# A decoder trunk's PEER layers: from gathered experts to both expert tables streamed through TensorE

## The chip, the core and the metric

The kernel runs on one core of a Trainium2 chip. A core has TensorE (PE in the rows: matrix products, with a separate weight-load stream PEld), VectorE (DVE), ScalarE (ACT), GpSimd (POOL) and SyncE (SP, which here only issues transfers), each with a queue of its own, and 16 DMA engines. SBUF is the on-chip memory of 128 partitions; PSUM is where TensorE leaves its products. The metric is device microseconds (us) of one execution, the median of several. The measurement can tell about 0.2% from no change.

## What is computed

A two-layer decoder trunk over 256 tokens of width 1024, all in float32. Layer 0 mixes tokens by sparse attention and retention, layer 1 by a convolution module; both are followed by a PEER block, and a last norm ends the trunk. PEER holds 16384 experts of one neuron each: a row of `u` (in) and a row of `v` (out), both 1024 wide.

```python
def peer_ffn(h, w_q, sub_keys, u, v):
    q = (xf @ w_q).reshape(T, P_HEADS, 2, P_QDIM // 2)          # T = 256, 8 heads, 2 x 128
    s1 = jnp.einsum('thd,kd->thk', q[:, :, 0], sub_keys[0])      # 128 keys each
    s2 = jnp.einsum('thd,kd->thk', q[:, :, 1], sub_keys[1])
    v1, i1 = lax.top_k(s1, 16); v2, i2 = lax.top_k(s2, 16)
    cand = (v1[..., :, None] + v2[..., None, :]).reshape(T, P_HEADS, 256)
    sv, ci = lax.top_k(cand, 16)
    eidx = (e1 * 128 + e2)                                       # 128 picks of a token
    gate = softmax(sv)
    hb = jnp.einsum('td,tkd->tk', xb, u[ib])
    act = jax.nn.gelu(hb) * gb
    return jnp.einsum('tk,tkd->td', act, v[ib])
```

Each token uses 128 experts of the 16384 in each layer (256 x 128 = 32768 picks a layer).

## The kernel before

The program is written engine by engine, with semaphores between them; the order on each engine is the order of the code. Tokens are worked in two tiles of 128 (`TILES`), and the PEER work in four phases `p`: layer 0 tile 0, layer 0 tile 1, layer 1 tile 0, layer 1 tile 1.

- **Picks.** `queries` (L1243) multiplies a head's 1024x256 slice of `wq` (loaded into `wbuf`, two buffers of 1 MB) with the transposed tokens `h_t`; ACT copies it to `q_t`; `scores` (L1254) multiplies with the keys; DVE's `heads` (L807) takes the top 16 of both score rows, the top 16 of their 256 sums, and turns them into expert numbers `eidx` and gates. One call of `heads` treats a pair of heads of one tile.
- **Experts.** `ring` holds 16 gathered rows for each token, 8 KB each (`u` and `v` side by side). GpSimd's `gathers` (L383) issues 512 indirect transfers (4 phases x 128 picks), each of one row for each of 128 tokens. DVE's `expert_round` (L879) makes the dot product with `u` (`dot`, L888) and adds half of the `v` row into `x_tok` (`add_v`, L896). ACT makes GELU times gate and a diagonal matrix of it (L558, L562, L569); TensorE adds the other half of the `v` row with that diagonal matrix (L1280).
- **Around it.** The heads of the next phase and layer 1's convolution for one tile are laid between expert rounds on every engine (`conv_pair`, L922, on DVE: 31 taps for each of 8 groups of 128 channels; `conv_beside` on PE and ACT). The output products of layer 0's tile 1 stand between rounds too (L1339). A norm is a square and a root on ACT, a multiplication by root and gain on DVE (L659, the gain row is loaded in 128 copies), a transposition on PE (L1027) and a copy on ACT (L431).
- **The start.** SP issues x, the first gain row, the parts of `w_in`, small tables, then `keys_sb` and `chan_sb` (L288, L289). PE's `product` (L1035) is a chain of 8 matmuls that add up over 1024 inputs.

In the rows a float32 matmul of the program appears as two records: 512 issued at L1280 are listed as x1024.

## Time and profile before

| | |
|---|---|
| median of 3 runs | 1693.82 us (1692.57 to 1694.78) |
| the profiled execution | 1694.12 us, of which the span of its core 1692.4 us |
| busy share of the span | DVE 84%, PE 58%, POOL 45%, PEld 35%, ACT 29% |
| moved | 625.78 MB, mean 370 GB/s; 536.90 MB of it gathered rows |
| granted TensorE clock, mean | 0.786 of full |

The profile has a page and views of the trace. The busy line gives each engine's share; the strips cut the span into 40 slices, a digit for each (9 is 90% or more, or nine tenths of the clock); the chain of work that ended last is followed back from the last instruction, step by step to what released it, so it says which engine set the time; the groups are instructions of one line and shape. The timeline lists instructions in order of time, merged when they are alike: start, length, engine, line, operation, count. For matmuls the length of a merged row includes the last one's way through the array, so the rate is read from start to start.

### The profile page before, as it was taken

To read this page: it belongs to the slowest core of one execution; us is meant where nothing else is said; L and a number is where in the kernel's file an instruction comes from. 1 tells how busy PE (TensorE), PEld (TensorE's weight loads), DVE (VectorE), ACT (ScalarE), POOL (GpSimd) and SP (SyncE) were. 2 spreads that over 40 slices of the span, in tenths; PEclk is the share of its full clock that TensorE was granted. 3 is DMA by queue.
4 is the path that set the end of the run, shared out by engine and by line. 5 is a ranking of instruction groups with operands and counts; after the bars stand their busy time and mean duration, and the time that the engine had idled before them with its cause. 6 is when DMAs were issued, how large, how long until landed. Compare 5 with 4: busy or idle time off the path is not lost.

```text
span 1692.4 us, 17116 instructions
## 1 busy us (share of the span) xinstructions
PE 983.0 (58%) x3934; PEld 597.7 (35%) x3934; DVE 1428.2 (84%) x3330; ACT 498.5 (29%) x1442; POOL 758.1 (45%) x565
## 2 busy tenths in 40 slices
PE   7999765444554634577444564557654446566555
PEld 7786443222331422344222342334332222122122
DVE  2755889999998989887999999986899999777776
ACT  2221332222223423333222333323332223232222
POOL 0002544433434587743433367734444336445541
PEclk9999877677777866798677787779877778877777
DMA  9146999999999978899999988889999989999996
GB/s 373 43 147 255 416 421 421 421 397 417 381 385 399 421 294 352 345 422 421 385 381 407 415 346 337 352 332 421 409 380 383 384 344 417 422 422 423 422 422 257
DMA packets 87274, 625.78 MB, mean 370 GB/s; under 512 B 9648, under 2 KB 10416, under 8 KB 12720
## 3 DMA queue, kind: packets, MB, share of 16 engines
q0 software_dynamic: 73728, 536.90, 77.7%
q1 hardware_dynamic: 13488, 88.20, 12.9%
q8 instruction: 24, 0.39, 0.1%
q14 instruction: 34, 0.28, 0.0%
HBM read 624.02 MB, written 1.05 MB: 369 GB/s over the span
## 4 chain that ended last, share of the span: by engine, by line
DVE 45%; PE 22%; DMA 14%; issue 11%; ACT 4%; DVEq 3%; ACTq 1%; POOL 0%; POOLq 0%
DVE ring L888 15%; DMA ring<-experts_dram,idx_now 12%; DVE x_tok L896 10%; PE side L1280 9%; PE pm L1038 8%; DVE conv_buf L939 7%; PE side L1038 2%; ACT act_v L562 1%; DMA wbuf<-w_dram 1%; DVE top_i L821 1%; DVE rest L822 1%; DVE top_i L834 1%; DVE best_i L840 1%; DVE side L843 1%; ACTq L565 1%
## 5 line engine op out<-in xcount | busy, mean ns | idle before, releaser
L410 POOL DMA_INDIRECT ring<-experts_dram,idx_now x512 | 728.0, 1422 | 680.0 <-DMA ring<-experts_dram,idx_now 309.6
L1280 PE MATMUL side<-ring,diag 128*128 128x512 f32 x1024 | 593.0, 733 | 598.7 <-ACT diag L569 598.5
L888 DVE SCALAR_TENSOR_TENSOR ring<-ring,h_tok 128x1024 f32<-128x1024 f32 x512 | 616.7, 1222 | 55.4 <-DMA ring<-experts_dram,idx_now 50.2
L1280 PEld LDWEIGHTS side<-ring,diag 128*128 128x128 f32 x1024 | 231.0, 237 | 904.7 <-ACT diag L569 668.5
L896 DVE SCALAR_TENSOR_TENSOR x_tok<-ring,act_v,x_tok 128x512 f32<-128x512 f32 x512 | 384.6, 751 | 26.1 <-ACT act_v L562 20.3
L558 ACT ACTIVATE ge<-hb 128x4 f32<-128x4 f32 x128 | 26.3, 205 | 696.6 <-DVE ring L888 696.6
L569 ACT ACTIVATE diag<-ident,act_v 128x128 f32<-128x128 f32 x512 | 163.8, 390 | 15.9 <-issue 2.3
L939 DVE SCALAR_TENSOR_TENSOR conv_buf<-conv_buf,chan_sb 128x128 f32<-128x128 f32 x480 | 126.7, 348 | 0.0
L1038 PEld LDWEIGHTS side<-h_t,wbuf 128*128 128x128 f32 x1024 | 119.3, 192 | 15.4 <-issue 15.4
L1038 PE MATMUL side<-h_t,wbuf 128*128 128x128 f32 x1024 | 119.5, 275 | 0.0
L562 ACT ACTIVATE act_v<-ge,gates 128x1 f32<-128x1 f32 x512 | 109.0, 283 | 15.5 <-issue 11.5
L393 POOL COPY idx_now<-eidx 128x16 uint32 x32 | 23.9, 745 | 170.8 <-DVE x_tok L896 97.0
L549 ACT ACTIVATE expo<-lead 128x16 f32<-128x16 f32 x32 | 6.7, 208 | 190.9 <-DVE lead L849 190.9
L1038 PEld LDWEIGHTS pm<-h_t,wbuf 128*128 128x128 f32 x512 | 59.7, 192 | 7.8 <-issue 7.8
L558 ACT ACT_TABLE_LOAD x46 | 59.0, 1283 | 3.4 <-issue 2.5
L1038 PE MATMUL pm<-h_t,wbuf 128*128 128x128 f32 x512 | 59.7, 275 | 0.0
L1038 PE MATMUL pm<-conv_buf,ring 128*128 128x128 f32 x448 | 53.7, 280 | 0.2 <-DVE ring L766 0.2
L1038 PEld LDWEIGHTS pm<-conv_buf,ring 128*128 128x128 f32 x448 | 52.3, 194 | 1.4 <-DVE ring L766 0.6
L1032 PE MATMUL pm<-ident,h_tok 128*128 128x128 f32 x56 | 12.8, 409 | 57.5 <-DVE h_tok L659 57.5
L888 DVE DVE_READ_ACCUMULATOR ring<-ring,h_tok 128x1 f32 x512 | 43.3, 85 | 0.0
L818 DVE MAX8 top_v<-side 128x8 f32<-128x128 f32 x64 | 15.6, 288 | 26.8 <-PE side L1259 26.8
L1038 PE MATMUL pm<-ring,conv_buf 128*128 128x512 f32 (+2 forms) x128 | 36.8, 445 | 1.1 <-ACT conv_buf L433 1.1
(188 smaller groups left out, 796.7 us busy)
## 6 DMA issues: line engine op xcount, KB each, us to landing
wbuf<-wq_dram SPq DMA_DIRECT2D x32, 1024.0 KB, 9.3
wbuf<-w_dram SPq DMA_DIRECT2D x24, 1024.0 KB, 9.5
ring<-w_in_dram SPq DMA_DIRECT2D x5, 2048.0 KB, 22.8
wbuf<-w_o_dram SPq DMA_DIRECT2D x8, 1024.0 KB, 8.3
ring<-experts_dram,idx_now POOLq DMA_INDIRECT x512, 11.5
gain<-gains_dram SPq DMA_DIRECT2D x7, 512.0 KB, 12.9
ring<-w_in_dram SPq DMA_DIRECT2D x1, 1696.0 KB, 9.8
x_tok<-x_dram SPq DMA_DIRECT2D x2, 512.0 KB, 4.8
```

The source lines that it names most:

```text
L393: pool.tensor_copy(idx_now[:, half, :], eidx[:, t, ds(i * (2 * RING) + half * RING, RING)]) \
L410: pool.indirect_dma_start(ring[:, r, :], None, table[layer], bass.IndirectOffsetOnAxis(idx_now[:, half, r:r + 1], 0)) \
L558: act.activation(ge[:, c], hb[:, c], ACT.Gelu)
L562: last = act.activation(act_v[:, r:r + 1], ge[:, r:r + 1], ACT.Copy, scale=gates[:, t, ds(i * RING + r, 1)])
L565: act.drain()
L569: act.activation(diag[:, (b % 2) * BATCH + j, :], ident[:, :], ACT.Copy, scale=act_v[:, r:r + 1]).then_inc(diag_ready, 1)
L821: dve.max_index(top_i[:, b, j, 0:8], top_v[:, b, j, 0:8], side[b, j])
L888: dve.scalar_tensor_tensor(out=ring[:, r, 0:D], in0=ring[:, r, 0:D], scalar=1.0, in1=h_tok[:, t, :], op0=ALU.mult, op1=ALU.mult, accum_out ...
L896: dve.scalar_tensor_tensor(out=xs, in0=ring[:, r, D:D + HALF], scalar=act_v[:, r:r + 1], in1=xs, op0=ALU.mult, op1=ALU.add).then_inc(v_add ...
L939: step = dve.scalar_tensor_tensor(out=dst, in0=src, scalar=tap, in1=dst, op0=ALU.mult, op1=ALU.add)
L1038: last = pe.matmul(dst, lhs(k), rhs(k), start=(k == 0), stop=(k == KD - 1))
L1280: pe.matmul(acc, diag[:, r % (2 * BATCH), :], ring[:, r, D + HALF:2 * D], start=False, stop=(last and r == RING - 1)) \
```

## The change

The phases are gone. A layer now takes its 256 tokens together, and all 16384 experts are evaluated for all of them. Expert number is e1 x 128 + e2; the tables are laid out on the host by e2.

- **U.** `expert_inputs`: 64 chunks of 1 MB a layer, each with the `u` rows of two values of e2 for all 128 values of e1. 16 matmuls (2 x 8, weights 128x128 of the table, 256 tokens moving) give 2 x 128 experts for 256 tokens in one PSUM bank; ACT applies GELU into `act`, which has a value for every expert and token (128 KB a partition).
- **Picks to gates.** DVE's `heads` now takes one head of both tiles; e1, e2 and the gate go to `picks`, are transposed once a layer (`transpose_picks`), and for each group of 8 tokens DVE builds one-hot matrices of e1 (`hot1`, 8x128) and of half the values of e2 (`hot2`, 8x64), GpSimd multiplies `hot2` by the gates, PE multiplies the two for each token (`gates_of_experts`: 8 matmuls of 64 moving columns, written to every 8th column of a PSUM bank), and DVE multiplies the result into `act` (`apply_gates`). A layer has 2 halves x 32 groups.
- **V.** `expert_outputs`: 64 chunks of 1 MB a layer, 8 matmuls each (2 tiles x 2 values of e2 x 2 halves of 512 columns, weights from `act`), added up in four PSUM banks over the layer; DVE adds them to `x_tok`.
- **Moved.** The convolution module treats 256 tokens at once and stands between the two PEER blocks with nothing beside it; the output products of tile 1 stand ahead of PEER. Gains are applied after the transposition, from `chan_sb` (one column for each 128 channels, L566), by DVE where ACT copied before. `chan_sb` is loaded second, `keys_sb` after all parts of `w_in`, and both add to the semaphore `small_loaded`. Weights and tables stream through `stream`, four buffers of 1 MB.

```diff
-    def gathers(p): ...                                     # 512 indirect DMAs
-    def expert_round(p, i, ...): ...                        # DVE, ACT and PE
+            def keep_h_t(e, dst):
+                dve.wait_ge(h_t_ps, e + 1)
+                g = CP_NORM + e // 2 * KD
+                dve.tensor_tensor(dst, norm_at(e).rearrange("p (k c) -> p k c", k=KD),
+                                  chan_sb[:, g:g + KD].unsqueeze(2).broadcast_to([P, KD, P]), ALU.mult).then_inc(h_t_ready, 1)
...
             norm(0)
             norm(1)
+            dve.wait_ge(small_loaded, 32)
+            keep_h_t(0, h_in[0])
+            keep_h_t(1, h_in[1])
...
+            def one_hots(i, half, g):
+                n = (2 * i + half) * GROUPS + g
+                if n >= 2:
+                    dve.wait_ge(gate_ps, n - 1)
+                dve.tensor_tensor(hot1[n % 2], iota..., picks_t[:, 0, tok]..., ALU.is_equal).then_inc(hot1_ready, 1)
+                dve.tensor_tensor(hot2[n % 2], iota..., picks_t[:, 1, tok]..., ALU.is_equal).then_inc(hot2_ready, 1)
...
+            def expert_inputs(i, c):
+                n = i * E_CHUNKS + c
+                w = chunk(C_U[i] + c).rearrange("p (k e c) -> p k e c", k=KD, e=E2_CHUNK)
+                if n >= 2:
+                    pe.wait_ge(gelu_ready, n - 1)
+                for e in range(E2_CHUNK):
+                    last = product(u_at[n % 2][:, e * TOKENS:(e + 1) * TOKENS], lambda k: w[:, k, e, :], lambda k: h_t[:, k, :])
+                last.then_inc(u_ps, 1)
...
+            def gates_of_experts(i, half, g):
+                n = (2 * i + half) * GROUPS + g
+                pe.wait_ge(hot1_ready, n + 1)
+                pe.wait_ge(gated_ready, n + 1)
+                if n >= 2:
+                    pe.wait_ge(gate_done, n - 1)
+                dst = gate_at[n % 2].rearrange("p (e u) -> p u e", u=GROUP)
+                for u in range(GROUP):
+                    last = pe.matmul(dst[:, u, :], hot1[n % 2][:, u, :], hot2[n % 2][:, u, :], start=True, stop=True)
+                last.then_inc(gate_ps, 1)
...
+            def expert_outputs(i, c):
+                for t in range(TILES):
+                    for e in range(E2_CHUNK):
+                        for k in range(2):
+                            last = pe.matmul(v_at[t][k], act[:, c * E2_CHUNK + e, t * P:(t + 1) * P], w[:, e, k * 512:(k + 1) * 512], ...)
...
+            def peer(i):
+                pe.wait_ge(h_t_ready, 4 + 4 * i)
+                queries(i, 0)
+                for h in range(1, P_HEADS):
+                    queries(i, h)
+                    scores(i, h - 1)
+                scores(i, P_HEADS - 1)
+                for c in range(E_CHUNKS // 2):
+                    expert_inputs(i, c)
+                transpose_picks(i)
+                for c in range(E_CHUNKS // 2, E_CHUNKS):
+                    expert_inputs(i, c)
+                    if c > E_CHUNKS // 2:
+                        gates_of_experts(i, 0, c - E_CHUNKS // 2 - 1)
+                gates_of_experts(i, 0, GROUPS - 1)
+                pe.wait_ge(gate_done, (2 * i + 1) * GROUPS)
+                for c in range(E_CHUNKS // 2):
+                    expert_outputs(i, c)
+                    gates_of_experts(i, 1, c)
+                pe.wait_ge(gate_done, (2 * i + 2) * GROUPS)
+                for c in range(E_CHUNKS // 2, E_CHUNKS):
+                    expert_outputs(i, c)
```

On DVE `peer(i)` is: eight `heads`, `normalise_gates` (waits for one Exp on ACT, which ACT has behind the GELU of chunk 31), the wait for the transposed picks, then for each half and group `one_hots` of the next group and `apply_gates` of this one.

On PE, where layer 0's experts begin, the program before has the diagonal products (L1280) with head work and output products (`pm<-wbuf,conv_buf`) between them:

```order
L1280 MATMUL side<-ring,diag 128x512 x4
L1038 MATMUL side<-h_t,wbuf 128x128 x16
L1280 MATMUL side<-ring,diag 128x512 x4
L1038 MATMUL side<-h_t,wbuf 128x128 x16
L1280 MATMUL side<-ring,diag 128x512 x4
L1259 MATMUL side<-keys_sb,q_t 128x128 x2
L1038 MATMUL pm<-wbuf,conv_buf 128x256 x8
```

The head work and the output products lie between the diagonal products here.

The changed program at the same place has the output products, the transposition of tile 1, eight heads, and then the first table:

```order
L928 MATMUL pm<-stream,mixbuf 128x256 x32
L922 MATMUL pm<-ident,h_tok 128x128 x8
L928 MATMUL side<-h_t,stream 128x256 x32
L1141 MATMUL side<-keys_sb,q_t 128x128 x4
...
L1141 MATMUL side<-keys_sb,q_t 128x128 x8
L928 MATMUL pm<-h_t,stream 128x256 x512
L1160 MATMUL side<-ident,picks 128x128 x6
L928 MATMUL pm<-h_t,stream 128x256 x32
L1172 MATMUL pm<-q_t,h_tok 128x64 x8
```

Every output product has moved ahead of the experts, and 512 matmuls on `u` stand in one row before anything waits for the picks. Further on, on PE of the changed program, where the second table begins (`big` holds `act`, `side` the sums):

```order
L928 MATMUL pm<-h_t,stream 128x256 x16
L1172 MATMUL pm<-q_t,h_tok 128x64 x16
L1182 MATMUL side<-stream,big 128x512 x8
L1172 MATMUL pm<-q_t,h_tok 128x64 x8
L1182 MATMUL side<-stream,big 128x512 x8
```

Two groups of gates stand together at the seam; before and behind it one group follows each chunk of a table.

At the start, on DVE, the program before has

```order
L655 RECIPROCAL rstd<-root 128x1
L659 SCALAR_TENSOR_TENSOR h_tok<-x_tok,rstd,gain 128x1024
L655 RECIPROCAL rstd<-root 128x1
L659 SCALAR_TENSOR_TENSOR h_tok<-x_tok,rstd,gain 128x1024
L672 RECIPROCAL rstd_y<-rstd_y 128x1
```

so that nothing stands between the two norms and the latents' norm, and the changed one has

```order
L557 RECIPROCAL rstd<-root 128x1 [waits norm_root]
L560 TENSOR_SCALAR h_tok<-x_tok,rstd 128x1024
L557 RECIPROCAL rstd<-root 128x1 [waits norm_root]
L560 TENSOR_SCALAR h_tok<-x_tok,rstd 128x1024
L569 TENSOR_TENSOR mixbuf<-pm,chan_sb 128x1024 [waits h_t_ps,small_loaded]
L569 TENSOR_TENSOR mixbuf<-pm,chan_sb 128x1024 [waits h_t_ps]
L587 RECIPROCAL stats<-stats 128x1 [waits ckv_root,uk_loaded]
```

The two multiplications by the gain (L569) are new on DVE, and the first waits for `small_loaded`.

## Rows read from the trace of the kernel before

**Rows 1.** The page: span, busy shares, granted clock in 40 slices, transfers.
```profile
span 1692.4 us, 17116 instructions
PE 983.0 (58%) x3934; PEld 597.7 (35%) x3934; DVE 1428.2 (84%) x3330; ACT 498.5 (29%) x1442; POOL 758.1 (45%) x565
PEclk9999877677777866798677787779877778877777
GB/s 373 43 147 255 416 421 421 421 397 417 381 385 399 421 294 352 345 422 421 385 381 407 415 346 337 352 332 421 409 380 383 384 344 417 422 422 423 422 422 257
DMA packets 87274, 625.78 MB, mean 370 GB/s; under 512 B 9648, under 2 KB 10416, under 8 KB 12720
q0 software_dynamic: 73728, 536.90, 77.7%
```
**Rows 2.** The page: the chain that ended last, its shares by engine.
```profile
DVE 45%; PE 22%; DMA 14%; issue 11%; ACT 4%; DVEq 3%; ACTq 1%; POOL 0%; POOLq 0%
```
**Rows 3.** The page: groups, count, busy us and mean ns, idle before and releaser.
```profile
L888 DVE SCALAR_TENSOR_TENSOR ring<-ring,h_tok 128x1024 f32<-128x1024 f32 x512 | 616.7, 1222 | 55.4 <-DMA ring<-experts_dram,idx_now 50.2
L896 DVE SCALAR_TENSOR_TENSOR x_tok<-ring,act_v,x_tok 128x512 f32<-128x512 f32 x512 | 384.6, 751 | 26.1 <-ACT act_v L562 20.3
L1038 PE MATMUL side<-h_t,wbuf 128*128 128x128 f32 x1024 | 119.5, 275 | 0.0
```
**Rows 4.** Timeline of PE: start, length (us), engine, line, what, records, idle before.
```profile
14.77 8.81 PE L1038 MATMUL pm<-ring,conv_buf 128*128 128x128 f32 x64 [1.10 <-ACT conv_buf L433]
...
61.87 13.90 PE L1038 MATMUL pm<-ring,conv_buf 128*128 128x512 f32 x32
75.61 1.04 PE L1173 MATMUL side<-ident,ring 128*128 128x128 f32 x8
...
109.45 5.92 PE L1038 MATMUL pm<-conv_buf,ring 128*128 128x128 f32 x48 [0.20 <-DVE ring L766]
...
167.79 0.86 PE L1133 MATMUL pm<-ident,ring 128*128 128x128 f32 x4 [2.20 <-DVE ring L752]
...
749.48 7.07 PE L1038 MATMUL pm<-wbuf,h_t 128*128 128x256 f32 x32
756.39 3.60 PE L1280 MATMUL side<-ring,diag 128*128 128x512 f32 x8
```
**Rows 5.** Groups of PE with shapes apart: the one with fewest moving columns.
```profile
L1038 PE MATMUL pm<-ring,conv_buf 128*128 128x8 f32 x32 | 3.7, 251 | 0.0
```
**Rows 6.** Stretches: length, busy (records) of PE and others, clock, DMA share, GB/s.
```profile
62.00:75.00 13.00, 13.00 (x32) 5.76 (x31) 9.73 (x17) 2.81 (x3) 0.40 (x1) 1.00 0.01 1
129.00:131.00 2.00, 2.00 (x4) 0.73 (x4) 1.78 (x7) 0.31 (x2) 0.00 (x0) 0.61 0.00 0
```
**Rows 7.** Timeline of DVE: one call of heads, its start, end of score reading, last instruction.
```profile
201.79 0.50 DVE L818 MAX8 top_v<-side 128x8 f32<-128x128 f32 x2 [3.59 <-PE side L1259]
...
204.67 0.87 DVE L827 MAX8 top_v<-rest 128x8 f32<-128x128 f32 x4
...
217.76 0.18 DVE L875 SCALAR_TENSOR_TENSOR eidx<-e 128x16 uint32<-128x16 f32 x1 [0.16 <-issue]
```
**Rows 8.** SP's queue: issue of the keys; then issues with KB each and us to landing.
```profile
11.27 0.71 SPq L288 DMA_DIRECT2D keys_sb<-keys_t_dram  x1
...
keys_sb<-keys_t_dram SPq DMA_DIRECT2D x1, 256.0 KB, 28.9
wbuf<-wq_dram SPq DMA_DIRECT2D x32, 1024.0 KB, 9.3
```
**Rows 9.** Timeline of DVE in the convolution of one tile: taps, reciprocal, scale and bias.
```profile
689.45 15.84 DVE L939 SCALAR_TENSOR_TENSOR conv_buf<-conv_buf,chan_sb 128x128 f32<-128x128 f32 x60
...
729.16 0.95 DVE L951 RECIPROCAL rstd_y<-rstd_y 128x128 f32<-128x128 f32 x1
...
731.49 2.14 DVE L956 TENSOR_SCALAR conv_buf<-conv_buf,chan_sb 128x128 f32<-128x128 f32 x8
```
**Rows 10.** Timeline at the end: the last sum is read, then norm and store.
```profile
1685.54 0.69 DVE L911 COPY x_tok<-side 128x512 f32<-128x512 f32 x1 [2.79 <-PE side L1280]
```

More of the change, by code:

```diff
@@ L73, in hybrid_decoder_trunk_kernel @@
     ds = bass.ds
-    wq_l = [wq[i, :, :, :] for i in range(LAYERS)]
-    table = [experts0, experts1]
+    u_l, v_l = [u0, u1], [v0, v1]
     ctx = ExitStack()
@@ L316, in load_chunks @@
-            def load_chunks(view, first, end, start=0):
-                for c in range(start, end):
+            sp.dma_start(row[:, :], b2.broadcast_to([P, D])).then_inc(row_loaded, 16)
+            def multiplied(n):
+                for i in (1, 0):
+                    if C_W1 <= n < C_WQ[1]:
+                        return (w2_ps, 4 + n - C_W2 + 1) if n >= C_W2 else (pw_ps, n - C_W1 + 1)
+                    if n >= C_V[i]:
+                        return v_used, i * E_CHUNKS + n - C_V[i] + 1
+                    if n >= C_U[i]:
+                        return u_ps, i * E_CHUNKS + n - C_U[i] + 1
+                    if n >= C_WQ[i]:
+                        return q_ps, i * P_HEADS + n - C_WQ[i] + 1
+                return wo_ps, 4 + n - C_WO + 1
@@ L520, in _ @@
             ps, done = read("c_t", 0)
[L521 removed]
+            sc.copy(c_t, ps[:, 0:SEQ]).then_inc(done, 1)
             relu_index(1)
@@ L828, in heads @@
                 dve.drain()
-                for b in pair:
+                for b in range(TILES):
                     dve.tensor_tensor(cand[:, b, :, :], top_v[:, b, 0, :].unsqueeze(2).broadcast_to([P, P_TOP, P_TOP]),
@@ L1322, in _, with scores @@
-            heads_start(0)
-            queries(0, 0, 0)
-            scores(0, 0, 0)
+            def scores(i, h):
+                n = i * P_HEADS + h
+                pe.wait_ge(q_t_ready, n + 1)
+                if n >= 2:
+                    pe.wait_ge(s_read, n - 1)
+                for t in range(TILES):
+                    for j in range(2):
+                        last = pe.matmul(s_at[h % 2][:, (2 * t + j) * P:(2 * t + j + 1) * P],
+                                         q_t[:, h % 2, j * TOKENS + t * P:j * TOKENS + (t + 1) * P], keys_sb[:, i, j, :], start=True, stop=True)
+                last.then_inc(s_ps, 1)
@@ new lines, in expert_outputs @@
+            def expert_outputs(i, c):
+                w = chunk(C_V[i] + c).rearrange("p (e c) -> p e c", e=E2_CHUNK)
+                first, end = c == 0, c == E_CHUNKS - 1
+                for t in range(TILES):
+                    for e in range(E2_CHUNK):
+                        for k in range(2):
+                            last = pe.matmul(v_at[t][k], act[:, c * E2_CHUNK + e, t * P:(t + 1) * P], w[:, e, k * 512:(k + 1) * 512],
+                                             start=(first and e == 0), stop=(end and e == E2_CHUNK - 1))
+                    if t:
+                        last.then_inc(v_used, 1)
+                    elif end:
+                        last.then_inc(v_ps, 1)
```

973 lines of the change are left out of this document (405 added, 568 removed).

## The prediction, made before the changed kernel was timed

> **What bounds the kernel now.** I read the page first, then the chain, the groups, and the timelines of the places that the change touches. The page [rows 1] shows DVE busy 84% of 1692.4 us and TensorE 58%, with a clock that is full in the first slices and lower behind them; 537 of 626 MB are gathered rows. The chain [rows 2] runs through DVE for 45%, PE 22% and DMA 14%: DVE paces, with the gathers close behind. The groups [rows 3] say with what: 512 dot products of 1.22 us and 512 half additions of 0.75 us, some 1000 us of DVE. TensorE's work is light and waits. So the old bound is a DVE pass over each gathered row. The change removes it whole; the question is what the dense work costs on TensorE.
>
> **The rates.** Everything hangs on how long TensorE takes for a float32 matmul, and the rows must be read from start to start, since two records stand for one matmul and a merged length has a tail. With 512 moving columns: 32 records from 61.87 to 75.61, 0.429 us each, 0.859 for a matmul [rows 4], at full clock [rows 6]. With 256 columns: 32 records from 749.48 to 756.39, 0.216 us each [rows 4]. With 128 columns 0.117 us [rows 3] and with 8 columns still 0.116 us [rows 5], so below 128 columns something other than the columns, the weight load beside it, sets 0.116. After an idle stretch the clock is lower for some microseconds (0.61 at 129 us, where four records took 2 us [rows 6]); dense stretches ran at 1.00.
>
> **The change, part by part.**
>
> *The start, +27.1.* PE's first projection begins at 14.77 [rows 4]. Now DVE multiplies the transposed tokens by the gain, and before the first of these it waits for the keys too, which SP issues last. They were issued at 11.27 and took 28.9 us [rows 8], so they landed at 40.2; about 0.35 MB less is ahead of them now, 0.8 us. Then two DVE passes over 1024 elements, 1.22 us each by L888 [rows 3], 0.1 for signals: PE starts at 41.9. All of PE, ACT and DVE is queued behind that wait, and nothing covers it. It could be less only if the keys overtook the weights; more, if the wait also cools the clock, at most 3 us.
>
> *Up to the first PEER block, 213.0.* The stretch between 109.45 and 167.79, where tile 1's retained values are transposed [rows 4], contained two head products of 32 records (3.7 us each at 0.117) and two calls of heads on DVE. They go; part of them lay under waits that remain, so I take 5.4 of the 7.5 us. What comes behind: transposition and copy 1.3, four output products of 16 records, 13.8, which had lain between expert rounds, an addition 0.4, and a norm with nothing beside it (square and root on ACT 2.9, DVE 1.5, transposition 2.0, gain 1.2, signals 0.4), 8.0. 167.8 - 5.4 + 23.5 + 27.1 = 213.0; 207 to 222 for the guesses in it.
>
> *Heads, 98 a layer.* A head is 16 matmuls of 256 columns, 6.9 us, and four of 128, 0.9 us. DVE's heads for one pair took from 201.34 (0.45 before the row at 201.79, for the two of its first four instructions that had gone ahead) to 217.94, 16.6 us; without the division, gates and expert numbers 15.4 [rows 7]. So DVE paces this stage: scores have two banks, and scores of head 7 wait until heads has read those of head 5. First scores at 16.9 (two products, cold clock 2.2, scores), then 5 x 15.4, then 3.3 until they are read (201.34 to 204.67 [rows 7]), then 0.9: 98. DVE ends heads some 42 us later, under the first of 32 chunks of U (221 us). If heads took 16.6, it is 104. The idle between products may halve the clock; the products would then take 15.6 us a head, as long as DVE: no more than a few us.
>
> *U, 442 a layer.* 64 chunks x 32 records x 0.216 = 442.2. A chunk of 1 MB every 6.9 us asks for 152 GB/s where the mean is now 370 [rows 1], issued three chunks ahead, 20.7 us, while one such transfer lands in 9.3 [rows 8]: hidden. GELU of 512 elements is below 1 us on ACT beside 6.9.
>
> *V, 440 a layer.* 64 x 16 records x 0.429 = 439.7, same transfers.
>
> *Gates, 119 a layer.* 64 groups x 16 records. No row has 64 columns; 8 and 128 both give 0.116 to 0.117, so 1.86 us a group. No row shows TensorE writing every 8th PSUM column either; see the second rival. DVE's part of a group, 1.2 (1024 elements) + 0.7 + 0.7 = 2.6 us, and GpSimd's 1 to 2, lie beside a chunk of 6.9; only the chunk covers them, and without it PE would wait some 5 us a group.
>
> *Seams, 7.4 a layer.* ACT makes the Exp of the gates behind the GELU of chunk 31: GELU 0.6, table change 1.3, Exp 0.4, three DVE passes 1.1, signals 0.2, and PE waits 3.6 for it, then 12 records of transposition, 1.4. Before each half of V, PE waits for the last `apply_gates`, 1.2 twice.
>
> A layer: 98 + 442.2 + 439.7 + 119.0 + 7.4 = 1106.3.
>
> *Convolution, 190, nothing beside it.* Additions and norm of both tiles 7.8. Two chunks of `w1` at 6.9, cold clock and gating 2.5: 16.3. Then DVE's 248 taps. For 128 columns 60 of them took 15.84, 0.262 apart [rows 9]; 128 elements more cost 0.12 to 0.15 by L888 and L896 [rows 3], so 0.395, 98.0, and six gatings 2.4. If the 0.262 were a floor of issue and not time per element plus a constant, it would be 0.333: 83. I take 0.395, since eight instructions without any wait took 2.14, 0.254 apart [rows 9]: the constant is there without the waits. Mean and variance on a cold PE 12.0; DVE and ACT between them 16.1 (the reciprocal was 0.95 for 128 columns [rows 9], 1.8 now); `w2` 128 records, 27.6 and 3 cold; additions and norm 6.6. Sum 190; 173 to 200.
>
> *End, 8.0.* From the read of the last sum to the end of the span were 6.9 [rows 10]; one more pair of additions and signals.
>
> **Sum.** 213.0 + 2 x 1106.3 + 190 + 8.0 = 2624 of span, and 1.7 outside it (1694.12 against 1692.4): 2625 us. The profiled run is 0.3 above the median, which is nothing here. TensorE's float32 work on the two tables alone, 1764 us, is more than the whole kernel before. Halving the bytes is worth nothing, since they were not what paced, and they are hidden twice over now.
>
> **Rivals.**
>
> *The table products are faster, and transfers pace: 1500.* Place: the records of U and V. If they were pulled together so that a chunk takes less than 2.5 us, the DMA engines, which reach about 420 GB/s in the slices [rows 1], would pace 268 MB of tables in 638 us: 2625 - 1764 + 638 = 1499. It decides below 3.3 us a chunk: fixed parts 2625 - 1764 = 861, (1694 - 861) / 256 = 3.25 us, where I have 6.9. Against it: 32 records in a row, without any wait, at 0.429 [rows 4]. Chance 2%.
>
> The Trainium skill has a rule that would give this: TensorE: Matmul & The Clock Gate, Back-to-back issue gap, gives a sustained 81 ns for a matmul of 128 columns and 131 ns for 512 in pairs with weight loads. Taken for a record, V would be 2.1 us a chunk and the whole about 1600. By that rule the kernel gets faster; the trace does not agree, with 429 ns for 512 columns. The same section's 512 / 2.4 + 2.5 is half of it.
>
> *Strided gate products are slow: 2830.* Place: the 1024 products of 64 columns written with a step of 8 through a whole bank. If a record costs as much as one of 256 columns, 0.216, it is 1.6 us more a group, 128 x 1.6 = 205: 2830. If it costs as one of 512 columns, the length of the bank that it spans, 128 x 5.0 = 641: 3266. It decides where a column written costs more than twice a contiguous one, since 64 columns leave half of 0.116 free. For it: no row at all. Chance 12%, most of it on the lower price.
>
> The Trainium skill speaks for this rival: SBUF — State Buffer, Door 1: The DMA port swizzle, says of PSUM that a non-contiguous access pattern significantly slows down matmuls. It names no factor, and no trace here shows it.
>
> *The V table's rows, 8 KB apart by half a megabyte, load slowly: 2820.* If a chunk took the 9.3 us of an issue to landing [rows 8] with no overlap, each V chunk alone would cost 2.4 more and each with gates 0.6: 128 x 1.5 = 192. Against: loads of the same size with large steps ran while gathers held the engines. 3%.
>
> *The clock does not hold in 450 us of dense products.* Each 1% of granted clock is 20 us. Against: 1.00 wherever it was dense; but no dense stretch of before was a quarter as long. 3%.
>
> **How the numbers follow.** My case has 80% and 2570 to 2680 by its own terms (start and convolution -25 to +19, heads +12, rates 1% either way, 20, and seams). That holds about seven in ten; the range must reach to the lower price of the strided products and to slow V loads, so it is 2570 to 2830. Faster by over 0.2% (about what a measurement can tell) 2%, within 0.2% next to nothing, 1%, slower 97%.
>
> **What would show it.** Right: PE over 90% busy from 310 us on at clock 1.00; U chunks 6.9 us from start to start, 8.8 with gates; V 6.9 and 8.7; no waits for `stream`; first projection at 42; convolution block 190 with DVE taps 0.39 apart. The claim falls if a record of 256 columns is not 0.216, if gate records are not 0.116, if a chunk's arrival ends PE's waits, or if DVE's heads do not pace the first 98 us of a block.

## The result, and the profile after

| | before | changed |
|---|---|---|
| median of 4 runs | 1693.19 us (1691.50 to 1694.78) | 2630.30 us (2624.29 to 2635.06) |
| profiled execution | 1694.12, span 1692.4 | 2635.06, span 2633.0 |
| ratio | | 1.5523, 95% interval 1.5488 to 1.5558 |

The changed kernel is 937 us slower; 2625 were forecast. The page of the changed kernel shows the new bound at once (busy us, share and instructions of each engine; granted clock and transfer rate in 40 slices; the chain):

```profile
PE 2417.9 (92%) x10306; PEld 1755.2 (67%) x10306; DVE 751.4 (29%) x1795; ACT 160.4 (6%) x249; POOL 141.6 (5%) x149
...
PEclk9999799999999999999996797999999999999999
...
DMA packets 44839, 320.96 MB, mean 122 GB/s; under 512 B 4928, under 2 KB 5696, under 8 KB 7104
...
PE 86%; DVE 10%; DVEq 1%; DMA 1%; ACT 1%; issue 1%; SPq 0%; ACTq 0%
```

Against [rows 1, 2]: half the bytes (321 MB for 626) at a third of the rate, DVE from 84% to 29%, and a chain that runs through PE for 86% instead of 22%. The groups of the changed kernel say with what (busy us, mean ns, idle before and its releaser); the first is U with the 256 records of the convolution's `w1`, the second V, the third the gates, the last DVE's part of the gates:

```profile
L928 PE MATMUL pm<-h_t,stream 128*128 128x256 f32 x4352 | 963.4, 383 | 1.3 <-DVE h_t L569 1.3
...
L1182 PE MATMUL side<-stream,big 128*128 128x512 f32 x2048 | 893.6, 594 | 3.1 <-DVE big L808 3.1
...
L1172 PE MATMUL pm<-q_t,h_tok 128*128 128x64 f32 x2048 | 242.2, 272 | 0.0
...
L808 DVE TENSOR_TENSOR big<-big,pm 128x512 f32<-128x512 f32 x128 | 88.0, 687 | 802.2 <-PE pm L1172 802.2
```

Without the 57 us of `w1`, U, V and gates hold PE for some 2040 us, and it waits for next to nothing in them: the second and third rows have 3.1 and 0.0 us of idle time before them, and DVE waits 802 us for the gates. The 512 + 512 passes of DVE over gathered rows [rows 3] are gone, some 1000 us, and what replaced them costs twice that on another engine.

The timeline of PE in the changed kernel shows each stage's seams (start, length, engine, line, what, records, idle before):

```profile
43.79 13.82 PE L928 MATMUL pm<-big,mixbuf 128*128 128x128 f32 x64 [30.40 <-DVE mixbuf L569]
57.47 6.14 PE L928 MATMUL pm<-mixbuf,big 128*128 128x128 f32 x32
...
225.98 15.85 PE L928 MATMUL side<-h_t,stream 128*128 128x256 f32 x64 [1.31 <-DVE h_t L569]
...
292.16 2.04 PE L1141 MATMUL side<-keys_sb,q_t 128*128 128x128 f32 x8 [5.65 <-DVE mixbuf L736]
...
322.97 2.05 PE L1141 MATMUL side<-keys_sb,q_t 128*128 128x128 f32 x8 [13.96 <-DVE mixbuf L736]
324.81 223.05 PE L928 MATMUL pm<-h_t,stream 128*128 128x256 f32 x1024
551.55 1.54 PE L1160 MATMUL side<-ident,picks 128*128 128x128 f32 x6 [3.70 <-DVE picks L789]
...
577.57 1.89 PE L1172 MATMUL pm<-q_t,h_tok 128*128 128x64 f32 x16
579.30 7.12 PE L928 MATMUL pm<-h_t,stream 128*128 128x256 f32 x32
586.26 1.89 PE L1172 MATMUL pm<-q_t,h_tok 128*128 128x64 f32 x16
...
834.14 7.13 PE L1182 MATMUL side<-stream,big 128*128 128x512 f32 x16 [0.78 <-DVE big L808]
841.11 1.89 PE L1172 MATMUL pm<-q_t,h_tok 128*128 128x64 f32 x16
...
1339.27 57.02 PE L928 MATMUL pm<-h_t,stream 128*128 128x256 f32 x256 [1.32 <-DVE h_t L569]
1455.89 6.63 PE L928 MATMUL side<-big,mean_w 128*128 128x256 f32 x16 [59.60 <-DVE big L850]
```

From start to start, as in the prediction: 32 records of a U chunk take 586.26 - 579.30 = 6.96 us, 16 gate records 579.30 - 577.57 = 1.73, a V chunk 841.11 - 834.14 = 6.97. These three numbers, 64 times each, are 1002 of the 1106 us that a PEER layer takes.

### The profile page after: what moved, and what is told of

Same layout as the page of the kernel before. It is cut to its first block, busy times and chain, and to the rows that moved or that the text cites. A ratio compares the mean times of both kernels' runs of the same rounds, so it can differ in the third digit from the quotient of the medians.

```text
span 2633.0 us, 23819 instructions
## 1 busy us (share of the span) xinstructions
PE 2417.9 (92%) x10306; PEld 1755.2 (67%) x10306; DVE 751.4 (29%) x1795; ACT 160.4 (6%) x249; POOL 141.6 (5%) x149
## 2 busy tenths in 40 slices
DMA packets 44839, 320.96 MB, mean 122 GB/s; under 512 B 4928, under 2 KB 5696, under 8 KB 7104
## 4 chain that ended last, share of the span: by engine, by line
PE 86%; DVE 10%; DVEq 1%; DMA 1%; ACT 1%; issue 1%; SPq 0%; ACTq 0%
PE pm L928 40%; PE side L1182 34%; PE pm L1172 8%; DVE big L850 4%; PE side L928 2%; DMA keys_sb<-keys_t_dram 1%; DVE top_i L735 1%; DVE mixbuf L736 0%; DVE top_i L746 0%; DVE best_i L752 0%; DVE mixbuf L755 0%; DVE top_v L732 0%; DVE best_i L763 0%; DVE mixbuf L769 0%; DVE mixbuf L773 0%
## 5 line engine op out<-in xcount | busy, mean ns | idle before, releaser
L928 PE MATMUL pm<-h_t,stream 128*128 128x256 f32 x4352 | 963.4, 383 | 1.3 <-DVE h_t L569 1.3
L928 PEld LDWEIGHTS pm<-h_t,stream 128*128 128x128 f32 x4352 | 829.4, 192 | 113.7 <-DVE h_t L569 1.7
L1182 PE MATMUL side<-stream,big 128*128 128x512 f32 x2048 | 893.6, 594 | 3.1 <-DVE big L808 3.1
L1182 PEld LDWEIGHTS side<-stream,big 128*128 128x128 f32 x2048 | 384.1, 190 | 461.9 <-issue 458.2
L1172 PEld LDWEIGHTS pm<-q_t,h_tok 128*128 128x128 f32 x2048 | 248.5, 192 | 33.8 <-issue 30.6
L364 POOL TENSOR_TENSOR q_t<-q_t,picks_t 128x512 f32<-128x512 f32 x128 | 137.2, 1072 | 2153.0 <-DVE q_t L800 2153.0
L1172 PE MATMUL pm<-q_t,h_tok 128*128 128x64 f32 x2048 | 242.2, 272 | 0.0
L798 DVE TENSOR_TENSOR h_tok<-iota,picks_t 128x1024 f32<-128x1024 f32 x128 | 155.9, 1218 | 5.1 <-ACT picks_t L505 5.1
L928 PE MATMUL side<-h_t,stream 128*128 128x256 f32 x512 | 120.4, 397 | 2.6 <-DVE h_t L569 2.6
L928 PEld LDWEIGHTS side<-h_t,stream 128*128 128x128 f32 x512 | 101.7, 201 | 17.9 <-DVE h_t L569 3.3
L1141 PE MATMUL side<-keys_sb,q_t 128*128 128x128 f32 x128 | 22.8, 335 | 56.8 <-DVE mixbuf L736 56.8
L928 PE MATMUL side<-big,mean_w 128*128 128x256 f32 x32 | 12.9, 590 | 63.9 <-DVE big L850 59.6
```

The source lines that it names most:

```text
L364: pool.tensor_tensor(hot2[n % 2], hot2[n % 2], picks_t[:, 2, g * GROUP:(g + 1) * GROUP].unsqueeze(2).broadcast_to([P, GROUP, E2_HALF]), AL ...
L798: dve.tensor_tensor(hot1[n % 2], iota[:, :].unsqueeze(1).broadcast_to([P, GROUP, P]), picks_t[:, 0, tok].unsqueeze(2).broadcast_to([P, GRO ...
L928: last = pe.matmul(dst, lhs(k), rhs(k), start=(k == 0), stop=(k == KD - 1))
L1141: last = pe.matmul(s_at[h % 2][:, (2 * t + j) * P:(2 * t + j + 1) * P], q_t[:, h % 2, j * TOKENS + t * P:j * TOKENS + (t + 1) * P], keys_s ...
L1172: last = pe.matmul(dst[:, u, :], hot1[n % 2][:, u, :], hot2[n % 2][:, u, :], start=True, stop=True)
L1182: last = pe.matmul(v_at[t][k], act[:, c * E2_CHUNK + e, t * P:(t + 1) * P], w[:, e, k * 512:(k + 1) * 512], start=(first and e == 0), stop ...
```

## The experiments

Every one is an edit of the changed kernel, and is compared with its 2630.30 us (and with the kernel before, which ran between them with medians of 1693 to 1695). The four runs of the changed kernel spread from 2624 to 2635, so a single run within that spread is no change.

### The shared count at the start

```diff
- sp.dma_start(keys_sb[:, :, :, :], keys_t).then_inc(small_loaded, 16)
+ sp.dma_start(keys_sb[:, :, :, :], keys_t).then_inc(keys_loaded, 16)
- dve.wait_ge(small_loaded, 32)
+ dve.wait_ge(small_loaded, 16)
  # PE, ahead of queries(i, 0)
+ pe.wait_ge(keys_loaded, 16)
```

> The keys get a count of their own, on which only TensorE waits, ahead of the first head; VectorE waits for the channel gains alone, which were issued first. My theory: the 29.0 us by which the first projection starts later in the changed kernel (43.79 instead of 14.77) are all this shared count, and the further 7.4 us lost by the time of 71.34 (before: 34.98, so 36.4 in all) are the slow stretch of TensorE after its 30.4 us wait. Both go: the first projection starts at 14 to 16 us, its records run as in the kernel before (64 in 8.7 us), and the kernel takes 2590 to 2597 us, a ratio of 0.985 to the changed kernel. Rival: the weights or the rotation tables, which queue on the same issuer, would be late in any case; the start then moves by less than 20 us and the kernel stays above 2610. Second rival: only the wait goes and the slow stretch stays, 2600 to 2605.

Measured: 2594.55 us (2592.42 to 2596.39, 4 runs), 1.5309 times the kernel before (1.5262 to 1.5355), so 35.8 us less than the changed kernel. PE's timeline of this run:

```profile
14.79 7.31 PE L929 MATMUL pm<-big,mixbuf 128*128 128x128 f32 x64 [1.31 <-DVE mixbuf L570]
...
187.21 15.85 PE L929 MATMUL side<-h_t,stream 128*128 128x256 f32 x64 [1.31 <-DVE h_t L570]
```

The first projection starts at 14.79, and its 64 records take 7.31 us, where the changed kernel's took 13.82. The first PEER block starts 38.8 us earlier. Nothing else that queues on SP is late: the keys alone were waited for. DVE's row in the changed kernel's trace names them:

```profile
41.38 2.36 DVE L569 TENSOR_TENSOR mixbuf<-pm,chan_sb 128x1024 f32<-128x1024 f32 x2 [30.38 <-DMA keys_sb<-keys_t_dram]
```

### Slow records behind the wait

The wait and the slow stretch behind it went together, so the slowness could have belonged to the idle time or to the place. Two runs keep the start at some 45 us and fill the wait with products of the identity that nobody reads.

```diff
              norm_h_t(1)
+             for n in range(105):      # 142 in the second run
+                 pe.matmul(side[:, 0, 0:P], ident[:, :], ident[:, :], start=True, stop=True)
              pe.wait_ge(h_t_ready, 2)
```

> TensorE fills its 30 us wait at the start with 105 products of the identity with itself, which nobody reads; all else is the changed kernel. My theory: the records after the wait are slow because TensorE idled ahead of them. Its first projection still starts at 43 to 45 us, but its 64 records take 7.3 to 8 instead of 13.8 us and the next 32 take 3.8 instead of 6.0; the kernel takes 2620 to 2628. Rival: it is the transfers that land in that stretch, or the weights' first use, that slow the records; they stay at 0.21 each.

Measured: 2637.66 us, one run. My expectation failed as written: the 105 products ended 8.4 us too early, and the slow records were still there. PE's timeline of this run:

```profile
13.38 23.79 PE L935 MATMUL side<-ident 128*128 128x128 f32 x210
45.60 13.82 PE L928 MATMUL pm<-big,mixbuf 128*128 128x128 f32 x64 [8.43 <-DVE mixbuf L569]
```

That left both explanations standing, so the gap was closed.

> The changed kernel with 142 products of the identity with itself in the wait at the start instead of 105, which had left TensorE 8.4 us idle ahead of its first projection, with the first 64 records still at 13.8 us. The 142 take 32 us by the measured 0.227 and leave no idle time. My theory: with no idle time before them, the 64 records take 7.3 to 8 us and the next 32 take 3.8. Rival: the idle time has nothing to do with it, and the records stay at 13.8 and 6 us; then the first use of that data or something in that stretch slows them.

Measured: 2627.85 us, one run. PE's timeline:

```profile
13.41 32.23 PE L935 MATMUL side<-ident 128*128 128x128 f32 x284
45.48 7.21 PE L928 MATMUL pm<-big,mixbuf 128*128 128x128 f32 x64
```

The same projection, at the same time, on the same data: 7.21 us without idle time before it and 13.82 with 8.4 us of it. Between these two runs only the idle time differs, so it is the cause of the doubling. The stretches of the runs say that this is the clock, though not in each of them (length; busy us and records of PE, PEld, DVE, ACT, POOL; granted clock, transfer share, GB/s). The first row is of the run with 105 products, the second of that with 142, the third of the changed kernel:

```profile
43.00:58.00 15.00, 12.40 (x59) 12.40 (x59) 2.87 (x4) 1.04 (x5) 0.00 (x0) 0.50 0.00 1
```

```profile
43.00:58.00 15.00, 15.00 (x137) 15.00 (x136) 3.15 (x6) 2.45 (x11) 0.00 (x0) 1.00 0.01 2
```

```profile
43.00:58.00 15.00, 14.21 (x66) 14.21 (x67) 1.25 (x3) 1.39 (x7) 0.00 (x0) 1.00 0.00 1
```

The first reads 0.50, the lower of the clock's two levels (1.2 GHz), the second the full 2.4 GHz. The third says 1.00, although its records took twice as long, as in the first. So a record's length is the better witness. The length of the slow stretch also varies from run to run after the same 30 us of idle time: the first 64 records took 13.8 us in the changed kernel's profile and 9.5, 9.1, 8.8, 8.8 and 8.7 in those of five variants that keep the wait. Some 9 us needs no long wait, though. With 1.3 us of idle time or less ahead of them the same records took 7.31 us in the run above and 8.81 in the kernel before, and in the run with both float32 edits (below):

```profile
14.73 9.06 PE L943 MATMUL pm<-big,mixbuf 128*128 128x128 f32 x64 [1.32 <-DVE mixbuf L584]
```

So the idle time made the long slow stretch possible and did not bring it every time. This is where most of the scatter of the changed kernel, 2624 to 2635, can come from: the two profiled runs with 13.8 us took 2635 and 2638 us, three float32 variants with 8.8 to 9.5 us took 2627 to 2629. The other runs have no trace, so that is argued and not shown. The Trainium skill (TensorE: Matmul & The Clock Gate, Seeing it yourself) warns that trace events of this clock have been unreliable; these stretches agree.

### Strided writes

Two edits, one for each direction of the same question. The first makes the contiguous U products strided:

```diff
- last = product(u_at[n % 2][:, e * TOKENS:(e + 1) * TOKENS], ...)
+ last = product(u_at[n % 2].rearrange("p (t e) -> p e t", e=E2_CHUNK)[:, e, :], ...)
  # and GELU reads u_at in that order
```

> The U products write their two experts' columns interleaved (step of 2 elements in the bank) instead of in two rows of 256, and the GELU reads with the same step. My theory: a strided write costs nothing, a U record stays at 0.216 us, a chunk at 6.91, the kernel at 2625 to 2636. Rival: a strided write slows the products; at half rate each of the 128 U chunks takes 13.8 us and the kernel takes 2630 + 128 x 6.9 = 3514 us; anything between shows as a chunk above 6.95. What may change in either case is the GELU (now 0.597), which lies beside 6.9 us of products and costs nothing below that. The Trainium skill, page on SBUF, section on the DMA port swizzle, says that a write to PSUM that isn't contiguous slows the matmul; by it, this kernel is the slower one.

Measured: 2628.74 us, one run. The second makes the strided gate products contiguous:

```diff
- dst = gate_at[n % 2].rearrange("p (e u) -> p u e", u=GROUP)
+ dst = gate_at[n % 2].rearrange("p (u e) -> p u e", u=GROUP)
  # and apply_gates reads gate_at in that order
```

> The 16 gate products of a step write 64 contiguous columns each, and it is VectorE's product with the GELU values that reads with a step of 64. My theory: the 16 products take the 1.73 us of the changed kernel (0.108 a record, strided by 16 elements) because a record of float32 has that floor whatever its columns are, and contiguous writes leave it at 1.70 to 1.75; the kernel stays within 0.3% of 2630. Rival: the stride costs, the step falls below 1.5 us, and with 128 such steps the kernel gains over 0.2 x 128 = 26 us. VectorE's product (now 0.687) may get longer by its strided read; VectorE has 2.5 of 8.6 us of work in a step, and this costs nothing.

Measured: 2627.28 us, one run. PE's timeline of the one with a step of 2 in U, and then of the one with contiguous gates:

```profile
571.57 1.89 PE L1172 MATMUL pm<-q_t,h_tok 128*128 128x64 f32 x16
573.29 7.13 PE L928 MATMUL pm<-h_t,stream 128*128 128x256 f32 x32
580.26 1.89 PE L1172 MATMUL pm<-q_t,h_tok 128*128 128x64 f32 x16
```

```profile
569.79 1.90 PE L1172 MATMUL pm<-q_t,h_tok 128*128 128x64 f32 x16
571.52 7.13 PE L928 MATMUL pm<-h_t,stream 128*128 128x256 f32 x32
578.49 1.90 PE L1172 MATMUL pm<-q_t,h_tok 128*128 128x64 f32 x16
```

A chunk takes 6.97 us in both, the 16 records of 8 gate products 1.72 and 1.73, as in the changed kernel. (The second expectation calls the records products and gives their step as 16 elements; it is 8.) Reading in the other order costs nothing either (GELU 0.60, DVE's product 0.69). The Trainium skill's rule that a non-contiguous PSUM pattern significantly slows down matmuls (SBUF — State Buffer, Door 1: The DMA port swizzle) doesn't hold for these float32 products, at steps of 2 and of 8 elements.

### The transfers

```diff
- sp.dma_start(stream[:, n % SLOTS, :], view[c, :, :])
+ sp.dma_start(stream[:, n % SLOTS, 0:CHUNK // 8], view[c, :, 0:CHUNK // 8])   # U and V chunks
```

> Of each U and V chunk only the first eighth of its columns is transferred, in the same number of transfers; the rest of the slot keeps what stood there, so the products are those of stale numbers, and 224 of the 256 MB of tables stay in HBM. All instructions are the same. My theory: TensorE is the limit, the chunks wait in their slots long before they are read, and the kernel stays within 0.3% of 2630 (2622 to 2638). Rival: the transfers cost something after all, by traffic into SBUF beside TensorE's reads or by late chunks; then a chunk falls below 6.91 and the kernel below 2615.

Measured: 2627.05 us, one run, with 86.08 MB moved instead of 320.96. That is within the changed kernel's spread: taking away 235 MB changes nothing that can be measured, and from bytes alone there is nothing to be had here.

### The heads

The timeline above has PE waiting for DVE in the heads. The group of the scores gives the sum over both layers, 56.8 us:

```profile
L1141 PE MATMUL side<-keys_sb,q_t 128*128 128x128 f32 x128 | 22.8, 335 | 56.8 <-DVE mixbuf L736 56.8
```

Five U chunks a layer are put into these waits:

```diff
- for h in range(1, P_HEADS):
-     queries(i, h)
-     scores(i, h - 1)
- scores(i, P_HEADS - 1)
+ for h in range(1, 6):
+     queries(i, h)
+     scores(i, h - 1)
+ queries(i, 6)
+ expert_inputs(i, 0)
+ expert_inputs(i, 1)
+ scores(i, 5)
+ queries(i, 7)
+ expert_inputs(i, 2)
+ scores(i, 6)
+ expert_inputs(i, 3)
+ expert_inputs(i, 4)
+ scores(i, 7)
  # the transfers and ScalarE in the same order
```

> Five U chunks a layer are placed between the last heads on TensorE (two behind the queries of head 6, one behind those of head 7, two before the last scores), on the transfers' issuer and on ScalarE alike; nothing else changes. My theory: VectorE's 15.4 us a head paces the heads, TensorE waits 3.8, 5.7, 4.5 and 14.0 us in them and runs its records slower after the waits; with the chunks between, only the 3.8 is left, the last U product of a layer ends 24 us of waits and about 6 us of slow records earlier, and the kernel gains 2 x 30 = 60 us: 2565 to 2577, a ratio of 0.977 to the changed kernel. Rival: the picks, not the U products, end last in the heads, since the transposes of the picks need VectorE's last head; with 27 chunks x 6.91 = 187 us of U products still ahead of them this rival gives no gain only if VectorE is later by that much. Second rival: the products between the heads delay VectorE's work on the scores, and the gain is below 30.

Measured: 2563.29 us (2556.55 to 2568.78, 4 runs), 1.5115 times the kernel before (1.5066 to 1.5164), 67.0 us less than the changed kernel, a ratio of 0.9745. That is beyond the end of my range. PE's timeline of this run:

```profile
219.34 16.44 PE L942 MATMUL side<-h_t,stream 128*128 128x256 f32 x64 [1.32 <-DVE h_t L583]
...
270.76 1.13 PE L1155 MATMUL side<-keys_sb,q_t 128*128 128x128 f32 x8 [3.78 <-DVE mixbuf L750]
...
324.44 186.65 PE L942 MATMUL pm<-h_t,stream 128*128 128x256 f32 x864
514.78 1.54 PE L1174 MATMUL side<-ident,picks 128*128 128x128 f32 x6 [3.69 <-DVE picks L803]
```

From the first query to the transposition of the picks it is 514.78 - 219.34 = 295.4 us, in the changed kernel 551.55 - 225.98 = 325.6: 30.1 less, as worked out, and the same stretch of layer 1 is 31.3 less. The rest lies elsewhere: this run's first block starts 6.6 us earlier than that of the changed kernel (219.34 for 225.98), with the same 30 us wait ahead of it but fewer slow records behind it.

Both edits together, in float32:

> The own count for the keys and five U chunks a layer among the heads, all in float32. My theory: the two gains lie in different stretches and add up: 2630 - 36 - 60 (the waits and slow records read from the trace) to 67 (the medians) = 2527 to 2534 us, 2520 to 2540. Rival: part of the 67 was the slow records at the start, which the own count takes away already; then it stays above 2535. Either way 64 x 6.9 + 64 x 6.9 + 64 x 1.73 = 994 us a layer of TensorE's float32 records stand, and no order of the work brings this form below 2 x 994 + 2 x 8 x 7.8 = 2113 us, above the kernel before.

Measured: 2534.66 us, one run, 95.6 less than the changed kernel. That is at the line between my sum (2527 to 2534) and the rival (above 2535), so the time alone doesn't decide; the traces do. Against the run with the keys' own count, the stretch from first query to transposition is 30.8 us shorter in layer 0 (483.74 - 188.90 for 512.80 - 187.21) and 31.3 in layer 1, as in the run before. So the heads' gain of some 62 us stands beside the start's, and the rest of the 67 was scatter at the start: here the first block starts 1.7 us later than with the own count alone.

### Float32 itself

What remains is what TensorE does with each product. So the table products are taken in bfloat16. ScalarE rounds each chunk into a second buffer, the transposed tokens once a layer, and the GELU values as it writes them.

```diff
+ sc.copy(low[:, c % SLOTS, :], stream[:, n % SLOTS, :]).then_inc(rounded, 1)
- last = product(u_at[n % 2][...], lambda k: w[:, k, e, :], lambda k: h_t[:, k, :])
+ last = product(u_at[n % 2][...], lambda k: w[:, k, e, :], lambda k: h_low[:, k, :])
  # w is low[...], act and h_low are bfloat16
```

> The products with the two expert tables are taken in bfloat16: ScalarE rounds each transferred chunk, the normalised rows and the GELU values (2048 elements a partition for a chunk), so these products and their result are less precise, while queries, scores, gates and all else stay in float32. My theory: TensorE's float32 records are the whole price of the dense form. With them at a quarter, the chunks go at the pace of ScalarE (two of its 1024-element copies of about 1.05 us and a GELU of 0.6: 2.6 us) or of the transfers (1 MB at the 428 GB/s of the start: 2.45 us) and, where a step has 16 gate products (1.73), at 1.73 + 1.73 = 3.5 us. A layer's two tables then take 32 x 2.6 + 32 x 3.5 + 32 x 2.45 + 32 x 3.5 = 386 us instead of 1007, and the kernel about 2630 - 2 x 621 = 1388 us, 1360 to 1500, below the kernel before. Rival: TensorE's time lies in its weight loads and not in its passes; then 16 loads a U chunk at the 0.192 of the profile's row hold it at 3.1 us and 6 or more with the gates, and the kernel takes over 1600.

Measured: 1389.71 us, one run: 1240.6 us less, and below the kernel before. The groups of this run's rounding on ScalarE and of U (busy us, mean ns, idle before):

```profile
L509 ACT CAST big<-stream 128x2048 bf16<-128x2048 f32 x256 | 484.6, 1898 | 150.0 <-PE side L1202 114.2
L946 PE MATMUL pm<-big 128*128 128x256 bf16 x2048 | 249.2, 277 | 29.6 <-ACT big L497 29.5
```

And PE's timeline of this run, in the second half of U:

```profile
471.20 1.91 PE L946 MATMUL pm<-big 128*128 128x256 bf16 x16
472.95 1.90 PE L1191 MATMUL pm<-q_t,h_tok 128*128 128x64 f32 x16
474.68 1.91 PE L946 MATMUL pm<-big 128*128 128x256 bf16 x16
```

A U matmul of 256 columns is now one record of 1.75 / 16 = 0.109 us where it was two of 0.216: a quarter. The step of a group of gates (16 records) and a chunk is 474.68 - 471.20 = 3.48 us instead of 8.69. The Trainium skill (FP8 and Floating Point Precision, TensorE Precision Notes) says that true float32 takes four passes through the array; the ratio measured here agrees.

With the other two edits, and with 12 instead of 5 chunks among the heads:

> The keys' own count, the table products in bfloat16 (less precise, as before), and twelve U chunks a layer among the heads, two with each head from the third. My theory: the three gains add up, since they lie in different stretches: 36 us at the start, and 12 chunks of 2.6 us in each layer's heads (62) besides the slow records there, from the time of the bfloat16 kernel: about 1388 - 36 - 62 = 1290 us, 1250 to 1390. Rival: ScalarE, which now rounds chunks and keeps queries in the same stretch, delays the queries, the heads get longer than 15.4 us each, and the gain is below half of that.

Measured: 1300.12 us, one run, 89.6 less than 1389.71 where I had worked out 98. One row of PE's timeline names what is left in the heads, a wait for DVE's last head in each layer:

```profile
286.05 2.05 PE L1176 MATMUL side<-keys_sb,q_t 128*128 128x128 f32 x8 [9.78 <-DVE mixbuf L771]
```

The gates, still in float32, are now half of each step they stand in. So their one-hot operands go to bfloat16 too:

```diff
- hot1 = [h_tok[:, n, :].rearrange("p (u c) -> p u c", u=GROUP) for n in range(2)]
+ hot1 = [h_tok[:, n, 0:D // 2].bitcast(b16).rearrange("p (u c) -> p u c", u=GROUP) for n in range(2)]
- hot2 = [q_t[:, n, :].rearrange("p (u c) -> p u c", u=GROUP) for n in range(2)]
+ hot2 = [q_t[:, n, 0:TOKENS].bitcast(b16).rearrange("p (u c) -> p u c", u=GROUP) for n in range(2)]
```

> The kernel before this one (own count for the keys, bfloat16 table products, twelve U chunks a layer among the heads) with the two one-hot operands of the gate products in bfloat16 too; the one-hots are exact in it, the gate values are rounded. There a step of 16 gate products and a chunk takes 3.47 us, half of it (1.73) the gates at 0.108 each. My theory: a float32 gate product has its 0.108 by the passes that float32 takes over its stationary 128 columns, and in bfloat16 falls to 0.03 to 0.06; the step then goes at VectorE's pace (1.22 + 0.71 + 0.69 = 2.6 us, less if bfloat16 makes it faster) or ScalarE's (1.9 + 0.6 = 2.5), and the kernel takes 1300 - 128 x 0.87 = 1189 us, 1150 to 1230. Rival: 0.108 is a floor of any product with a freshly loaded 128-column operand; the step stays at 3.47 and the kernel at 1290 to 1305.

Measured: 1205.36 us (1204.20 to 1208.66, 4 runs), 0.7116 times the kernel before (0.7104 to 0.7128). The timelines of PE and DVE in one step of this kernel:

```profile
400.27 1.94 PE L963 MATMUL pm<-big 128*128 128x256 bf16 x16
402.65 0.61 PE L1208 MATMUL pm<-q_t,h_tok 128*128 128x64 bf16 x8 [0.45 <-issue]
403.07 1.94 PE L963 MATMUL pm<-big 128*128 128x256 bf16 x16
```

```profile
401.96 1.68 DVE L833 TENSOR_TENSOR h_tok<-iota,picks_t 128x1024 bf16<-128x1024 f32 x1
403.56 0.68 DVE L835 TENSOR_TENSOR q_t<-iota,picks_t 128x512 bf16<-128x512 f32 x1
404.16 0.68 DVE L843 TENSOR_TENSOR big<-big,pm 128x512 bf16<-128x512 bf16 x1
404.76 1.68 DVE L833 TENSOR_TENSOR h_tok<-iota,picks_t 128x1024 bf16<-128x1024 f32 x1
```

PE's step is 403.07 - 400.27 = 2.80 us and DVE's 404.76 - 401.96 = 2.80 without a gap: DVE sets the pace. A gate product is one record now where it was two, as with U: the 8 products of a group take 403.07 - 402.65 = 0.42 us, 0.052 each, where the 16 records of float32 took 1.73, 0.216 a product. (The expectation takes records for products; its 0.108 is half a product.) So the price goes with the type, to a quarter as for U, and is no floor that every product of this shape has. Whether the weight load or the pass of the columns sets it is not shown, since both are in the same type: the mean weight load of these products fell too, from 0.192 to 0.118 us.

The steps went from 3.48 and 3.46 us (with a chunk of U and of V) to 2.80, not to the 2.6 that I had worked out, because DVE's comparison with 1024 results got slower with a bfloat16 output: 1.60 us from start to start where it was 1.13 with a float32 output. 128 steps account for 86 us of the gain of 94.8; the other 9 are not followed up.

These last kernels are less precise than the reference in the layers' tables. They show what the limit is and where it goes next; they are no replacement where float32 is asked for.

## Why the prediction was right, point by point

The sum had 2624 us of span, the profiled run, the slowest of the four, 2633.0. The mechanism came out as told: TensorE's float32 records pace U, V and the gates, and DVE paces the heads and the convolution. By the terms of the sum:

| term | predicted | measured |
|---|---|---|
| start to first PEER block | 213.0 | 225.98 |
| heads, layer 0 | 98 | 98.8 |
| U with gates and seams, layer 0 | 507.9 | 509.3 |
| V with gates and seam, layer 0 | 500.4 | 497.9 |
| convolution with the norms around it | 190 | 188.6 |
| layer 1's block | 1106.3 | 1104.9 |
| end | 8.0 | 7.5 |

- **The rates** carried the forecast, and they came from rows of before: 0.216 us for a record of 256 columns and 0.429 for 512 [rows 4], read from start to start. After: 6.96 / 32 = 0.218 and 6.97 / 16 = 0.436 for a chunk taken alone between gates, and V's total of 497.9 us fits 0.431. The mean ns of the groups, 383 and 594, would have misled, since pipelined records overlap.
- **The gates** were 0.108 a record and not 0.116: 16 x 64 x 0.008 = 8 us less in a layer. The row of 8 columns [rows 5] and that of 128 [rows 3] were both a little above. By the prediction's own words the claim falls if gate records are not 0.116; they were not, and the forecast stood because they are under a tenth of the time. In U the saving was used up, by luck and not by the working: PE is busy 504.9 us there, and 442.2 + 55.4 + 1.4 are 499.0. Of the 5.9 us between, 2.1 are slow records behind the wait for the picks (the 64 records from 552.89 took 15.99 us, at a granted clock of 0.86). The stretches of heads, U and V of layer 0 in the changed kernel, columns as above:

```profile
225.98:324.81 98.83, 70.93 (x320) 61.62 (x321) 76.82 (x328) 5.98 (x9) 0.00 (x0) 0.85 0.24 86
324.81:834.14 509.33, 504.85 (x2568) 450.28 (x2567) 117.91 (x253) 42.05 (x69) 34.28 (x32) 0.99 0.38 132
834.14:1332.04 497.90, 497.12 (x1536) 251.73 (x1536) 79.64 (x98) 2.03 (x3) 34.30 (x32) 1.00 0.38 133
```

- **The start is the term that was mis-sized.** The wait for the keys was found, and its cause; 27.1 became 29.0. The keys landed at 41.4 where 39.4 was worked out. What the prediction gave "at most 3 us", the clock cooled by that wait, cost more in the profiled run: the block starts 38.8 us earlier with the wait gone, so 9.8 us were slow records, 8.8 of them in the 112 records right behind the wait and 0.9 in a later stage. In the five variants with the same wait and 8.7 to 9.5 us for the first 64 records, the "at most 3" holds; the profiled run had the long stretch. So the first block's 225.98 lies outside the 207 to 222 that the prediction gave it. Without the start's 27.1 the prediction had 185.9 for the first block, the run without the wait has 187.2. The 13.0 us of that line are 1.9 of wait, 9.8 of slow records and 1.3 of all the rest.
- **Heads** are paced by DVE: 15.4 us a head, with PE waiting 5.6 and 14.0 us in the rows above, and filling the waits gave back 30 us a layer.
- **Seams**: 3.70 us for the Exp (3.6) and 0.78 for the last gates (1.2).
- **Convolution**: 60 taps took 23.84 us, 0.396 apart (0.395), and PE waits 59.6 us for them. The block is 181.3 us, and the norm ahead of it 7.2. The sign that PE is over 90% busy from 310 us on does not hold in this stretch and in layer 1's heads.

The rivals: **transfers pace** needed a chunk below 3.25 us; it is 6.96, and an eighth of the bytes changes nothing. In bfloat16 it comes near: V's chunks without gates start 2.48 us apart, where the slices of the page show 421 GB/s. **Strided gates** cost nothing, by both edits; this was the largest rival (12%), and no row of before could settle it. **V's rows load slowly**: a V chunk lands a median 4.7 us after its issue, as a U chunk does (4.8), and V's group above has 3.1 us of idle time, all of it on DVE and none on a transfer. **The clock doesn't hold**: 1.00 over the 498 us of V.

## What to carry to other kernels

Read a float32 matmul's price from start to start of long runs of records before exchanging bytes for products: here it is 0.43 us for 128x128 by 256 and decides all, since the kernel before was paced mainly by DVE, with 14% of its chain on transfers and 22% on TensorE. An edit that puts an engine's first work behind a later transfer costs the wait and, in some runs, a slow clock behind it; give each transfer its own count. In float32 the dense form's records add up to some 2 x 1000 us at the measured rates, whatever the order of the work. In bfloat16 the dense form takes 29% less time than the gathering one in float32; the gathering form in bfloat16 was not tried, so that is no comparison of the two forms at one precision.

## What the runs showed of the hardware that was not expected

- 8.4 us of idle time ahead of a projection came with 64 records at twice their length (13.8 us for 7.2), and the same records ran at full pace when the idle time was filled. After some 30 us of idle time the slow stretch lasted differently long in each run, 8.7 to 13.8 us for these records; with 1.3 us ahead they took 7.3 to 9.2. The granted clock of the view could read 1.00 through a slow stretch.
- A float32 gate product of 64 columns takes 0.216 us (two records of 0.108), in bfloat16 0.052 (one record).
- Float32 products written to PSUM with a step of 2 or 8 elements cost the same as contiguous ones.
- DVE's comparison of float32 operands with 1024 results had a mean of 1.22 us with a float32 output and 1.64 with a bfloat16 one; the one with 512 results did not change (0.71).
